# RMS-norm factors applied behind the projections, and the transposes of the activations moved into the neighbouring products

## What is computed

```python
def rmsnorm(x, g):
    return x * lax.rsqrt(jnp.mean(x * x, axis=-1, keepdims=True) + EPS) * g

# layer 0
z = rmsnorm(x, norm_mix[0]) @ w_in_even          # 2048 -> 5376: k, v, q | gates, u, v of the spatial gate
mixed = concat(silu(ga) * window_attention(q, k, v), silu(gb) * spatial_gate(u, vb))
x = x + mixed @ w_out_even
x = x + cross_attend(rmsnorm(x, norm_cross[0]) @ w_xq, mem_k, mem_v) @ w_xo
# layer 1: retention with 8 heads
q, k, v, g = split(rmsnorm(x, norm_mix[1]) @ w_in_ret)
x = x + (silu(g) * standardize(retention(q, k, v))) @ w_out_ret
x = x + cross_attend(rmsnorm(x, norm_cross[1]) @ w_xq, mem_k, mem_v) @ w_xo
# memory keys and values of each layer, from 256 memory tokens
mem_k, mem_v = rmsnorm(mem, norm_mem[l]) @ w_xk, rmsnorm(mem, norm_mem[l]) @ w_xv
y = rmsnorm(x, norm_final)
```

## Time and profile before

| | us |
|---|---|
| median of 3 runs (lowest, highest) | 3578.32 (3578.22, 3584.36) |
| profiled execution | 3580.66 |
| its span, first to last instruction | 3578.9 |
| TensorE busy | 3350.0 (94%) |
| TensorE weight loads (beside it) | 2633.4 |
| GpSimd busy | 1065.0 (30%) |
| VectorE busy | 988.0 (28%) |
| ScalarE busy | 959.8 (27%) |
| mean granted TensorE clock | 0.974 of 2.4 GHz |

### The profile page before, as it was taken

The page is one execution under the profiler, slowest core; times in us unless marked ns, Lnnn a source line. Parts: engine busy times, 40 slices in busy tenths (PEclk is TensorE's granted clock), DMA queues, the critical chain, the costliest instruction groups (busy, mean ns, idle before and its releaser), DMA issues.

```text
span 3578.9 us, 43292 instructions
## 1 busy us (share of the span) xinstructions
PE 3350.0 (94%) x15505; PEld 2633.4 (74%) x15505; DVE 988.0 (28%) x1720; ACT 959.8 (27%) x1471; POOL 1065.0 (30%) x444
## 2 busy tenths in 40 slices
PE   6799999999998789999999999999999989999886
PEld 5687777777877678686777767686767768788765
DVE  3501244233212451313222231303132240212225
ACT  4422334233223232121312222121212131212232
POOL 5542322322332023132322223232323223333211
PEclk9999999999999899999999999999999999999988
DMA  7333221223222233333333333333333343422222
GB/s 248 107 96 97 67 68 57 66 74 119 80 82 92 87 108 101 124 115 119 120 111 107 114 118 109 119 119 121 117 115 123 119 159 130 135 72 81 77 93 84
DMA packets 211716, 380.35 MB, mean 106 GB/s; under 512 B 20448, under 2 KB 59232, under 8 KB 207520
## 3 DMA queue, kind: packets, MB, share of 16 engines
q1 hardware_dynamic: 137744, 233.34, 21.3%
q10 hardware_dynamic: 73824, 144.84, 12.1%
HBM read 318.95 MB, written 60.16 MB: 106 GB/s over the span
## 4 chain that ended last, share of the span: by engine, by line
PE 71%; DVE 8%; ACT 1%; issue 1%; DVEq 1%; ACTq 0%
PE bank L547 16%; PE bank L549 16%; PE bank L548 16%; PE bank L551 4%; PE bank L552 4%; PE bank L563 2%; DVE R L1775 2%; PE bank L880 2%; PE bank L582 2%; PE bank L871 2%; DVE R L1773 1%; PE bank L919 1%; PE bank L915 1%; PE bank L911 1%; DVEq L1510 1%
## 5 line engine op out<-in xcount | busy, mean ns | idle before, releaser
L524 POOL TENSOR_TENSOR w_lo<-w_raw,w_hi 128x1024 fp32r<-128x1024 f32 x440 | 1064.8, 2421 | 2468.5 <-ACT w_hi L977 2468.1
L547 PE MATMUL bank<-w_hi,xT_hi 128*128 128x512 f32 (+1 forms) x2880 | 1166.3, 405 | 38.4 <-ACT R L1199 17.4
L549 PE MATMUL bank<-w_hi,xT_lo 128*128 128x512 f32 (+1 forms) x2880 | 1122.9, 390 | 0.0
L548 PE MATMUL bank<-w_lo,xT_hi 128*128 128x512 f32 (+1 forms) x2880 | 1121.8, 390 | 0.0
L977 ACT ACTIVATE w_hi<-w_raw 128x1024 fp32r<-128x1024 f32 x440 | 465.5, 1059 | 1737.4 <-PE bank L552 1628.6
L547 PEld LDWEIGHTS bank<-w_hi,xT_hi 128*128 128x128 f32 x2880 | 545.4, 189 | 182.5 <-issue 29.0
L548 PEld LDWEIGHTS bank<-w_lo,xT_hi 128*128 128x128 f32 x2880 | 546.0, 190 | 115.3 <-issue 11.5
L549 PEld LDWEIGHTS bank<-w_hi,xT_lo 128*128 128x128 f32 x2880 | 544.7, 189 | 115.1
L551 PE MATMUL bank<-w_hi,xT_sample 128*128 128x512 f32 (+1 forms) x816 | 328.8, 403 | 5.4 <-DVE R L1773 4.8
L552 PE MATMUL bank<-w_lo,xT_sample 128*128 128x512 f32 (+1 forms) x816 | 316.8, 389 | 0.0
L989 ACT ACTIVATE R<-bank 128x512 f32<-128x512 f32 (+6 forms) x342 | 180.0, 532 | 399.0 <-PE bank L563 262.0
(11 more groups left out here) (172 smaller groups left out, 2270.5 us busy)
## 6 DMA issues: line engine op xcount, KB each, us to landing
w_raw<-in_w_in_ret SPq DMA_DIRECT2D x128, 512.0 KB, 3.7
w_raw<-in_w_in_even SPq DMA_DIRECT2D x80, 512.0 KB, 3.6
w_raw<-in_w_in_ret SPq DMA_DIRECT2D x128, 256.0 KB, 2.9
R<-in_state_ret ACTq DMA_DIRECT2D x64, 512.0 KB, 4.6
out_ret_state_sample<-R ACTq DMA_DIRECT2D x64, 512.0 KB, 3.1
w_raw<-in_w_out_ret SPq DMA_DIRECT2D x64, 512.0 KB, 3.6
w_raw<-in_w_out_even SPq DMA_DIRECT2D x32, 512.0 KB, 3.6
mix_scratch<-R ACTq DMA_DIRECT2D x16, 576.0 KB, 3.5
```

Of the source, the lines that this page charges most:

```text
L524: pool.tensor_tensor(wlo[:, s], raw[:, s], whi[:, s].bitcast(F32), ALU.subtract).then_inc(lo_ready, 1)
L547: pe.matmul(acc, th[:, k, tok], hi[:, kk, 0:width], start=first, stop=False)
L548: pe.matmul(acc, th[:, k, tok], lo[:, kk, 0:width], start=False, stop=False)
L549: mm = pe.matmul(acc, tl[:, k, tok], hi[:, kk, 0:width], start=False, stop=last)
```

## The change

- The gains of six norms are loaded as small rows, transposed once, and lie as columns in `gT`. The gain is now applied where the transposed activations are split into high and low part (the `scale` of ScalarE's copy; a scalar operand on VectorE).
- rstd is applied to the projection's result when it leaves PSUM (`scale_of(t)`, `sample_sum`). The diagonal matrices and `norm_tile` go; transposes are plain (`tp`, one instruction a block).
- X is transposed column chunk by column chunk inside the next product: when chunk i of the output projection has been added to X, its four 128-column strips and the sample tile are transposed at given steps of chunk i + 1 (`EARLY`, `THIRD`, `BRIEF`), the last ones in the following query chunk (`FOURTH`). Where the old activations are still in use, the result is first staged in SBUF (`stg`) and split later. The weight groups of some chunks come in the order `GORD`. The memory tokens and x for n0 are transposed inside the memory chunks; those of zt inside eout's first chunk (`ZT_STEPS`).
- In the retention heads the gates have four buffers; the four Silus stand ahead of the root, and the sample tile's behind it. `RA_POINTS` and `RZ_POINTS` come some steps later.
- The loops of pair3, eout and the second half of rout are unrolled; the squares' unused output goes to SBUF instead of bank 7.

```diff
-XT_BANKS = [5, 6, 7, 0, 1, 2]
+XT_BANKS = [5, 6, 7]
+GORD = [4, 5, 0, 1, 2, 3, 6, 7]
+EARLY = {8: 0, 13: 1, 18: 2, 23: 3, 28: 4}
+FOURTH = {5: 0, 9: 1, 13: 2, 17: 3, 21: 4}
+BRIEF = {4: 0, 5: 1, 6: 2, 7: 3, 8: 4}
+THIRD = {13: 0, 18: 1, 23: 2, 28: 3, 31: 4}
...
-RA_POINTS = [(4, "M00"), (8, "M01"), (12, "M02"), (18, "M10"), (22, "M11"), (26, "M12")]
-RZ_POINTS = [(2 + 3 * n, name) for n, (_, name) in enumerate(RA_POINTS)]
+RA_POINTS = [(9, "M00"), (13, "M01"), (17, "M02"), (22, "M10"), (26, "M11"), (30, "M12")]
+RZ_POINTS = [(6 + 3 * n, name) for n, (_, name) in enumerate(RA_POINTS)]
...
-        QK, V, ON, sg = c.take(5, CW), c.take(5, CW), c.take(5, CW), c.take(2, CW)
+        QK, V, ON, sg = c.take(5, CW), c.take(5, CW), c.take(5, CW), c.take(NT, CW)
...
+            def xt_k(stage, k, src):
+                pe.wait_ge(*is_free(stage, ("xt", k)))
+                bk = bank_of(stage, ("xt", k))
+                for t in range(NT):
+                    mm = tp(bk[:, t * P:(t + 1) * P], src[:, t, k * P:(k + 1) * P])
+                mm.then_inc(FULL(stage, ("xt", k)), 1)
...
+            def column_step(stage, source, i, c, points, step):
+                if step not in points:
+                    return
+                j = points[step]
+                tag, i = source[1](i)
+                if j == 0:
+                    for t in range(NT):
+                        pe.wait_ge(*is_drained(source[0], (tag, t), i))
+                if j < 4:
+                    xt_k(stage, 4 * c + j, X)
+                else:
+                    pe.wait_ge(*is_drained(source[0], (tag, NT), i))
+                    xt_s(stage, ("s", c), X, 4 * c, 4)
...
             def cross(l):
                 st = f"x{l}"
-                norm(st, 9 + 10 * l)
-                xt_done(st, 18)
-                gemm(Lin(plan.groups[st + "q"]), st, "acc")
+                gemm(Lin(plan.groups[st + "q"]), st, "acc", between=lambda step: query_step(l, step))
...
+            def hi_k(stage, k, gains):
+                act.wait_ge(*is_full(stage, ("xt", k)))
+                bk = bank_of(stage, ("xt", k))
+                kw = dict(scale=gain(gains, k)) if gains else {}
+                copy(xh[:, k, :], bk[:, :], **kw).then_inc(xt_hi_ready, 1)
...
             def c_evac(stage, h, i):
                 act.wait_ge(*is_full(stage, "OI", i))
                 copy(ON[0:NS, NT], bank_of(stage, "OI")[0:NS, :]).then_inc(FREE(stage, "OI"), 1)
+                for t in range(NT):
+                    act.wait_ge(*is_full(stage, ("C", t), i))
+                    act.wait_ge(gated, 5 * (1 + h) + (t + 1))
+                    act.activation(sg[:, t], bank_of(stage, ("C", t))[:, :], ACT.Silu, scale=scale_of(t)).then_inc(FREE(stage, ("C", t)), 1)
                 act.wait_ge(var_ready, plan.st["gn"] + 1 + h)
-                act.activation(stat[:, 101:106], stat[:, 96:101], ACT.Sqrt).then_inc(std_ready, 1)
-                gate_evac(stage, "C", i, 2 + h, sg, sgs)
+                act.activation(stat[:, 74:79], stat[:, 51:56], ACT.Sqrt).then_inc(std_ready, 1)
+                act.wait_ge(*is_drained(stage, ("C", NT), i))
+                act.activation(sgs[0:NS, :], sgs[0:NS, :], ACT.Silu).then_inc(sil_ready, 1)
...
+            def lo_k(stage, k, gains):
+                v.wait_ge(xt_hi_ready, plan.hi[stage, k] + 1)
+                bk = bank_of(stage, ("xt", k))
+                if gains:
+                    ins = v.scalar_tensor_tensor(xl[:, k, :], bk[:, :], gain(gains, k), xh[:, k, :].bitcast(F32), ALU.mult, ALU.subtract)
...
             def sample_sum(dst, bk, ins_sem, width=CW):
-                do(v.tensor_copy(dst, bk[0:NS, 0:width]))
-                do(v.tensor_tensor(dst, bk[NS:2 * NS, 0:width], dst, ALU.add).then_inc(ins_sem, 1))
+                do(v.tensor_scalar(dst, bk[0:NS, 0:width], stat[0:NS, 94:95], None, ALU.mult))
+                do(v.scalar_tensor_tensor(dst, bk[NS:2 * NS, 0:width], stat[NS:2 * NS, 94:95], dst, ALU.mult, ALU.add).then_inc(ins_sem, 1))
```

More of the change, by code:

```diff
@@ L218, in make_plan @@
     sqrt("n0", 1)
-    xt("n0", 18)
+    late = []
+    for g in range(1, GPC):
+        late += [(1, g - 1)] + ([("s", g // 2)] if g % 2 else [])
+    xt("n0", [(0, g) for g in range(GPC)] + late + [(1, GPC - 1)])
+    late = []
+    for g in range(1, GPC):
+        late += [(1, g - 1)] + ([] if g % 2 else [("s", g // 2 - 1)])
+    highs("n0", [(0, g) for g in range(GPC)] + late + [(1, GPC - 1), ("s", 3)])
+    splits("n0", [("s", c) for c in range(4)])
     weights("even", 11)
@@ L252, in make_plan @@
             sqrt("n1", 1)
-            xt("n1", 18)
+            for n in range(4):
+                xt("n1", columns(n))
+                highs("n1", columns(n))
+                splits("n1", [("s", n)])
             weights("ret", 3 * RH)
@@ L442, in rows, with gain, scale_of @@
             return P if t < NT else NS
+        def gain(name, k, n=1):
+            at = KT * GAINS.index(name) + k
+            return gT[:, at:at + n]
+        def scale_of(t):
+            return stat[0:rows(t), 90 + t:91 + t]
         block = ctx.enter_context(nc.Block())
@@ L470, in _ @@
                     chunk(Lin(base + GPC * (3 + 2 * pair), GPC, i), w, col + CW * i)
-            with sp.Fori(0, 4) as i:
-                chunk(Lin(plan.groups["eout"], GPC, i), I.w_out_even[0], CW * i)
+            for i in range(4):
+                chunk(Lin(plan.groups["eout"] + GPC * i), I.w_out_even[0], CW * i, order=GORD)
             def cross(l):
@@ L499, in _ @@
             head(RH - 1, Lin(base + GPC + 3 * GPC * (RH - 1)))
-            for half in range(2):
-                with sp.Fori(0, 4) as i:
-                    chunk(Lin(plan.groups["rout"] + 4 * GPC * half, GPC, i), I.w_out_ret[0], CW * i, k0=KT * half)
+            with sp.Fori(0, 4) as i:
+                chunk(Lin(plan.groups["rout"], GPC, i), I.w_out_ret[0], CW * i)
+            for i in range(4):
+                chunk(Lin(plan.groups["rout"] + (4 + i) * GPC), I.w_out_ret[0], CW * i, k0=KT, order=GORD if i == 3 else range(GPC))
             cross(1)
@@ L528, in _, with gemm @@
         def _(pe):
-            def gemm(L, stage, tag, i=0, tiles=ALL, width=CW, groups=GPC, g0=0, between=None, parts=(xh, xl)):
+            def gemm(L, stage, tag, i=0, tiles=ALL, width=CW, groups=GPC, g0=0, between=None, parts=(xh, xl), order=range(GPC), k0=0):
                 th, tl = parts
@@ new lines, in xt_s, with xt_ready @@
+            def xt_s(stage, name, src, k0, n):
+                pe.wait_ge(*is_free(stage, ("xt", name)))
+                bk = bank_of(stage, ("xt", name))
+                for j in range(n):
+                    mm = tp(bk[:, j * NS:(j + 1) * NS], src[0:NS, NT, (k0 + j) * P:(k0 + j + 1) * P], NS)
+                mm.then_inc(FULL(stage, ("xt", name)), 1)
+            def xt_ready(stage, *names):
+                for name in names:
+                    pe.wait_ge(*is_drained(stage, ("xt", name)))
@@ new lines, in _, with n0_step @@
+            for ch in range(4):
+                l = ch // 2
+                gemm(Lin(plan.groups["mem"] + GPC * ch), "mem", ch, tiles=[2 * l, 2 * l + 1], between=lambda step: mem_step(ch, step))
+            xt_half("n0", (1, GPC - 1), X[:, 2:4], GPC - 1)
+            def n0_step(step):
+                g, n = divmod(step, PT)
+                if n == 0:
+                    xt_ready("n0", (0, g), (1, g))
+                elif n == NT and g % 2 == 0:
+                    split_ready("n0", ("s", g // 2))
@@ L1002, in xt_all, with hi_half @@
-            def xt_all(stage, tiles):
-                n = 0
-                for t in tiles:
-                    for q in range(4 if t < NT else 2):
-                        xt_hi(stage, n, t, q)
-                        n += 1
+            def hi_half(stage, name, g, tok, gains):
+                act.wait_ge(*is_full(stage, ("xt", name)))
+                bk = bank_of(stage, ("xt", name))
+                for kk in range(GK):
+                    k = GK * g + kk
+                    ins = copy(xh[:, k, tok:tok + 256], bk[:, kk * 256:(kk + 1) * 256], scale=gain(gains, k))
+                ins.then_inc(xt_hi_ready, 1)
@@ L1115, in kvq_evac @@
             def kvq_evac(ch):
+                if ch == 0:
+                    rstd(2)
                 for t in range(NT):
```

648 lines of the change are left out of this document (415 added, 233 removed).

## The result

The changed kernel takes 3491.4 us (median of four, 3490.8 to 3495.2) where the kernel before takes 3580.5 in the same comparison: ratio 0.9752, 95% interval 0.9735 to 0.9769. I had forecast 3480 within 3452 to 3505. The profiled execution took 3490.97, span 3489.2; the forecast made against the profiled execution was 3482.5, so the gain was over-estimated by 8.5 us. The kernel before took 3579.05 to 3580.5 us in the different comparisons, so 1 to 2 us of a difference between them mean nothing.

What follows compares the result with a forecast made beforehand. TensorE, busy 94% of the span, bounds the kernel, so its idle time and non-projection work can be won. Gains 138.7 less losses 40.5, net 98.2 us, took the profiled 3580.66 to 3482.5, median 3480 us, range 3452 to 3505.

Steps and rivals of the forecast that it cites:

- The heads: Seven retention head ends: late root frees bank 4 late, one 6.6 us TensorE wait, lower clock; 5.5 each, 38.5 us lost.
- The last head: After the last retention head: wait moves from tile 0 to the sample tile, M00's cover goes; 2 us lost.
- The norm boundaries: Starts at x0, n1, x1: waits and norm matmuls go, transposes come inside products; 24.4, 24.5, 25.3 us won.
- residual waits: Residual additions lose their gain multiply, and with it most of the sample tile's waits: 3 of 4.8 us won.
- zt: Before eout: 72 transposes and waits leave, most strips return inside the chunk; net 2.5 us won, bounds 0 and 5.
- The start: Memory phase: first product at 16, nothing on TensorE waiting for squares, root or gain, kvq at 120.3; 56 us won.
- kvq and pairs: In kvq the rescaling L1610 falls into the PSUM exit: 3 of its 3.4 us of wait won.
- (a): Rival: retention heads gain as four buffers promise, 17.2 us won instead of 38.5 lost; about 3420 us, chance 0.08.
- (b): Rival: retention heads lose only the 3.25, without the clock loss; 3465 us, inside the forecast's own range.
- (c): Rival: new waits at strip banks, memory-phase weights, x0's output, eout's start; all 3505 us; chance 0.17 for 3495 to 3520.
- (d): Rival: transposes strewn in products hold TensorE at 1.2 GHz, 503 us more, 3983 us; chance 0.03.
- 128 us and 3556: By the Trainium skill's 275 ns per transpose, 464 blocks cost 128 us instead of 51; forecast would be about 3556.

Runs made afterwards that it cites:

- The first experiment: Changed kernel with the gains' columns and first three half strips ahead of weight groups 2 and 3 on ScalarE; 3491.0 us, ratio 0.9749.
- the early sum: Changed kernel with VectorE adding up the gate chunk's sample tile while it waits for the root, ahead of the group norm's factors; 3435.2 us, ratio 0.9601.

## Why the forecast was right, and where its terms were not

**The heads** (forecast 38.5 lost, measured 40.2 over the seven). Each step held: the root late, bank 4 as the limit, tiles 0 to 3 in 5.5 us, a wait of 6.6 (measured 6.97), the lower clock behind it. Two sizes were off and nearly cancel. The four Silus take 2.42 us, 0.6 each and not 0.54, so against the gate chunk's last matmul the root ends 3.3 us later than before and not 2.95; the new sum adds 0.1. And the lower clock held for 7 to 10 matmuls, 9 as a mean of the seven heads, and not for 12: about 1.8 us instead of 2.2. With M00's 0.35 that makes 5.6 of the 5.74 measured per head. Three runs show that this part is the cause: by itself it costs 34 us on the old kernel, taking it back wins 44, and moving the root alone wins 30 of these 44. The other 14 belong to the four buffers and the helpers' places, which no run separates.

**The last head** (forecast 2 lost, measured 5.5). The wait moved from tile 0 to the sample tile as I said, 10.33 us. The sample tile's first product comes 16.2 us behind the gate chunk's last matmul in both kernels; what is lost behind it is the clock (ten matmuls, 2.1 us), M00's 0.35, and a new wait for VectorE's residual addition at the output projection's second chunk:

```profile
2859.99 0.80 PE L610 MATMUL bank<-w_hi,xT_sample 128*128 128x512 f32 x1 [10.33 <-DVE R L1868]
...
2911.60 0.50 PE L606 MATMUL bank<-w_hi,xT_lo 128*128 128x512 f32 x1 [1.01 <-DVE R L2076]
```

Also lost here are 1.5 us within the gate chunk: a wait of 2.4 us that both kernels have was followed by matmuls at half clock in the new one only. This I couldn't have read from the trace before.

**The norm boundaries** (forecast x0 24.4, n1 24.5, x1 25.3, residual waits 3, zt 2.5; together 79.7, measured 31.6 + 23.9 + 30.4 = 85.9). The blocks are gone, four transposes cost 0.44 as counted, VectorE didn't hold up the short chunks of x0's output projection. zt came out as worked: eout starts at 802.0, ahead by 60.1, 10.6 more than at pair3's end (10.5 forecast). The 6 us above the forecast lie in the two cross attentions, which the change doesn't touch: from their first transposes to their output projection they take 77.2 and 77.3 us instead of 81.0 each, 7.5 in all, and their matmuls ran at a higher granted clock. The same stretch of x1, before and after:

```profile
3422.00:3444.00 22.00, 16.66 (x93) 13.14 (x91) 8.82 (x17) 11.80 (x29) 2.36 (x1) 0.92 0.35 114
```

```profile
3336.90:3357.00 20.10, 14.28 (x89) 11.10 (x88) 9.28 (x17) 11.21 (x28) 2.36 (x1) 1.00 0.35 112
```

Both begin with the same transposes and end at the same product; the work takes 1.6 us less (3422.77 to 3444.49 against 3336.86 to 3357.01) at a granted clock of 1.00 instead of 0.92. What sets the clock in such a stretch of short waits I can't say from these runs.

**The start** (forecast 56, measured 44.1) is the step that failed, in the prediction's words "12.1 + 0.6 + 1.1 + 1.4 + 0.5 = 15.7, say 16". The sentence before it, that nothing on TensorE waits for the gain, was wrong: TensorE waits 6.98 us for the gain columns. I took the landing of the memory tokens as the last condition and did not look at what stands ahead of the gain copy on ScalarE's queue: four weight copies, of which the last waits for a transfer that now shares the way with x, requested at 5.25 instead of behind the squares (15.49 before). That is 8.5 us. The other 3.5 are the exit of the first chunk waiting for its norm factor (2.5), and the rest of the memory phase. The first experiment also shows that mending the queue alone would not have given the 8.5: the weights and the norm factor stood right behind it. My price of nothing for GpSimd working beside VectorE was wrong at the same place: I asked if GpSimd would be slowed down, and it is VectorE that is held up.

**kvq and pairs** (forecast 3, measured 5.4): the wait for L1610 went; the rest is kvq's start at full clock (its first 24 matmuls take 2.9 us instead of 5.3), which I had left out.

**The total** came nearer than its terms. The start gave 12 us less than forecast and the heads took 5 more; the norm boundaries and kvq gave 9 more, of which most is granted clock that I did not foresee. That these nearly made up for each other was luck.

**The rivals.** (a), heads that gain, is out. (b), no clock loss, is out: granted clock 0.51. Of (c) the start's part came true in size. (d), transposes that hold the clock down, is out: 1.00 over 160 us of eout with 735 instructions. So the Trainium skill's statement that a transpose doesn't count as busy for the clock gate in the same way ("TensorE: Matmul & The Clock Gate", Part 4: PE-mode transpose) changes nothing visible when four of them stand between 28 matmuls. Its 275 ns for one is a duration, and there the trace agrees: 272 ns as a median. But transposes overlap, and one adds 0.11 us from start to start. The prediction's 128 us and 3556, and its remark that the trace doesn't go by the page, took that duration for the price.

## What to carry to other kernels

Work that is moved off the critical engine keeps its own queue: before an instruction with a long consumer chain (here the root) is put behind others, ask which bank or buffer the end of that chain releases, and what the consumer does until then. If a chain can't be made shorter, take the release out of it: the early sum empties bank 4 in time that VectorE had idle, and is worth 56 us where the order of the root is worth 30. And count a wait that goes away as work that starts beside something else: with TensorE no longer standing, GpSimd ran beside VectorE and stretched its standardizing from 3.04 to 6.88 us.
